# Recalls in four parts, upper weight halves on GpSimd and a new order for the opening of a hybrid decoder kernel

## The reference, cut to what matters

```
h = rmsnorm(x) * norm_pre
c = h @ w_in                       # 1024 -> 3600 columns, split in groups of 256 and a low rank one of 16
A: gated linear attention, 4 heads, log_a = log_sigmoid(a_lr @ gla_w_a2 + b) / 16
C: the same recurrence with k = sigmoid(-c_f), log_f = log_sigmoid(c_f), q = silu(c_q)
   S_t = diag(exp(log_a_t)) S_{t-1} + k_t v_t^T ;  o_t = S_t^T q_t ; o = head_rmsnorm(o)
B: b_b * conv3(b_c * b_v)          D: (trailing means over 2/4/8/16 - d_v) @ pool_w * pool_scale
mix = concat(A, B, C, D), each times silu of its own gate a_z, b_z, c_z, d_z
x = x + rmsnorm(mix @ w_out) * norm_post
```

## Time and profile before

| what | value |
|---|---|
| time, median of 3 runs | 980.12 us (979.66 to 980.3) |
| the profiled execution, its own time | 980.61 us |
| its span, first to last instruction | 978.8 us |
| busy in the span | PE 951.4, DVE 614.2, ACT 431.0, POOL 357.8 us |
| TensorE enters the loop over tiles 2 to 7 | 176.64 us |

### The profile page before, as it was taken

How to read it: one execution, slowest core, us unless ns; L and a number is a source line. 1 busy time by engine, 2 the same in 40 slices (tenths; PEclk the granted TensorE clock), 3 DMA queues, 4 the chain that set the end, 5 groups by cost and what they waited for, 6 DMA issues and landing times.

```text
span 978.8 us, 23985 instructions
## 1 busy us (share of the span) xinstructions
PE 951.4 (97%) x10276; PEld 712.0 (73%) x10276; DVE 614.2 (63%) x1051; ACT 431.0 (44%) x833; POOL 357.8 (37%) x456
## 2 busy tenths in 40 slices
PE   4999999999999999999999999999999999999997
PEld 3777768856887678856887678856887678856783
DVE  5989887437754576537753576537853577447654
ACT  7966355333643334523543434523543435424323
POOL 1315550168004650177103650077103660067300
PEclk9997799999999999999999999999999999999999
DMA  9910432001220104001220104001220013001101
GB/s 332 338 63 3 155 116 72 1 1 45 66 65 2 44 24 109 1 1 44 67 66 1 44 24 108 2 1 45 62 70 1 26 42 87 1 1 45 66 7 44
DMA packets 41547, 56.06 MB, mean 57 GB/s; under 512 B 27808, under 2 KB 28633, under 8 KB 41433
## 3 DMA queue, kind: packets, MB, share of 16 engines
q1 hardware_dynamic: 41441, 54.53, 17.7%
HBM read 38.46 MB, written 9.86 MB: 49 GB/s over the span
## 4 chain that ended last, share of the span: by engine, by line
PE 70%; DVE 14%; ACT 8%; DMA 3%; issue 3%; POOL 1%; SPq 0%; DVEq 0%; ACTq 0%; POOLq 0%
PE pj L873 35%; PE op L1160 16%; PE pj L892 8%; DVE A L2194 3%; PE sc L963 2%; DMA wo_hi<-in_w_units 2%; DVE xres L2087 2%; ACT xres L1501 1%; ACT w_hi L1472 1%; PE sc L1180 1%; PE op L1180 1%; DMA h<-xres 1%; PE m L1072 1%; DVE xres L2448 1%; DVE X L2419 1%
## 5 line engine op out<-in xcount | busy, mean ns | idle before, releaser
L873 PE MATMUL pj<-h,w_hi 128*128 128x256 f16 (+1 forms) x3456 | 385.4, 265 | 3.5 <-DVE w_lo L2065 3.2
L873 PEld LDWEIGHTS pj<-h,w_hi 128*128 128x128 f16 x3456 | 310.6, 99 | 53.5 <-issue 10.0
L873 PE MATMUL pj<-h,w_lo 128*128 128x256 f16 (+1 forms) x1728 | 209.1, 264 | 0.0
L873 PEld LDWEIGHTS pj<-h,w_lo 128*128 128x128 f16 x1728 | 158.2, 99 | 17.5
L2194 DVE COPY_PREDICATED A<-cu8w,sc 64x384 f32<-64x384 uint8 (+1 forms) x168 | 74.0, 440 | 34.6 <-PE sc L963 31.3
L714 POOL TENSOR_TENSOR G<-B 128x256 f32<-128x256 f32 x17 | 12.8, 756 | 176.7 <-DVE B L2120 165.3
L2184 DVE COPY A<-sc 64x256 f32<-64x256 f32 x28 | 11.8, 421 | 87.1 <-PE sc L963 86.9
L892 PE MATMUL pj<-w_hi,h 128*128 128x512 f16 (+1 forms) x272 | 63.3, 379 | 0.0
L730 POOL TENSOR_TENSOR G<-G,Q 128x256 f32<-128x256 f32 x17 | 13.5, 793 | 113.9 <-ACT K L1452 100.0
L2412 DVE SCALAR_TENSOR_TENSOR X<-X 128x512 f32<-128x512 f32 x32 | 22.2, 692 | 50.0 <-ACT X L1452 46.6
L1160 PE MATMUL op<-wo_hi,m_hi 128*128 128x512 f16 x224 | 53.0, 379 | 0.0
(11 more groups left out here) (355 smaller groups left out, 1655.2 us busy)
## 6 DMA issues: line engine op xcount, KB each, us to landing
xin<-in_x_prompt SPq DMA_DIRECT2D x16, 512.0 KB, 4.1
wo_hi<-in_w_units SPq DMA_DIRECT2D x16, 512.0 KB, 7.6
xres<-in_x_prompt SPq DMA_DIRECT2D x15, 512.0 KB, 3.5
out_y_prompt<-xres SPq DMA_DIRECT2D x14, 512.0 KB, 2.6
wo_lo<-in_w_units SPq DMA_DIRECT2D x12, 512.0 KB, 6.6
xres<-in_w_out SPq DMA_DIRECT2D x8, 256.0 KB, 3.1
gpost<-in_w_out SPq DMA_DIRECT2D x8, 256.0 KB, 2.9
m_hi<-in_x_prompt SPq DMA_DIRECT2D x1, 512.0 KB, 5.5
```

Source lines behind the costliest of these rows:

```text
L873: m = pe.matmul(b[:, j * T:(j + 1) * T], w[:, k, col + 128 * j:col + 128 * j + 128], h[:, k, :], start=(n == 0 and k == 0), stop=(n == 2 a ...
```

## The change

Three things. `recall` takes a list of parts, and for tile 0 each of four parts does a quarter of the matmuls, with other work between them. The upper halves of six pieces of w_in (6, 9, 12, 15, 18, 21) are made by GpSimd with a `tensor_scalar` of its own (`upper_helped`), counted by a semaphore of its own; TensorE and SyncE now wait for the lower halves alone, which come after the upper ones. And the lists of all engines for the opening, up to the loop over tiles 2 to 7, are in a new order. The loop and what follows are untouched. The diff, cut where the lists go on in the same manner:

```diff
@@ -69,10 +69,10 @@
 
 def fill_order():
     fills = [
-        (0, "lr"), (0, "la"), (0, "a_k"), (0, "a_q"), (1, "lr"), (1, "la"), (1, "a_q"), (1, "a_k"),
-        (0, "c_f"), (0, "tin"), (0, "vi0"), (0, "c_q"), (1, "c_f"), (1, "c_q"), (0, "d_v"), (1, "vi0"),
-        (0, "d_z"), (1, "vi1"), (0, "po"), (0, "a_z"), (0, "c_z"), (0, "b_c"), (0, "b_v"), (0, "b_z"),
-        (0, "tails"), (0, "b_b"), (1, "d_v"), (1, "d_z"), (1, "po"), (1, "a_z"), (1, "b_c"), (1, "b_v"),
+        (0, "lr"), (0, "la"), (0, "a_k"), (0, "a_q"), (1, "lr"), (1, "la"), (1, "a_q"), (0, "c_f"),
+        (1, "a_k"), (0, "c_q"), (0, "tin"), (1, "c_f"), (0, "vi0"), (0, "d_v"), (1, "vi0"), (1, "c_q"),
+        (0, "d_z"), (0, "po"), (0, "a_z"), (0, "c_z"), (1, "vi1"), (0, "b_c"), (0, "b_v"), (0, "b_z"),
+        (0, "tails"), (0, "b_b"), (1, "d_v"), (1, "d_z"), (1, "po"), (1, "b_c"), (1, "a_z"), (1, "b_v"),
         (1, "b_b"), (1, "b_z"), (2, "lr"), (2, "la"), (1, "c_z"),
...
@@ -140,9 +140,22 @@
     return (0 if name in OWN0 else FIRST.get(name, SIGNALS[name])) + (i - 1) * SIGNALS[name] + k
 
 
+HELPED = (6, 9, 12, 15, 18, 21)
+
+
 def converted(u):
 
     return 2 * u + 2 if u < 4 else u + 5
+
+
+def uppers(u):
+
+    return converted(u) - sum(1 for h in HELPED if h <= u)
+
+
+def helped(u):
+
+    return HELPED.index(u) + 1
 
 
 def needed(col):
...
             def unit(u):
 
                 if u >= NSTAGE:
-                    sp.wait_ge(once["whi"], converted(u - NSTAGE))
                     sp.wait_ge(once["wlo"], converted(u - NSTAGE))
                 sp.dma_start(stage[u % NSTAGE], a["w_units"][u].rearrange("p (k n) -> p k n", k=2)
                              ).then_inc(once["wld%d" % (u % NSTAGE)], 16)
@@ -763,6 +775,14 @@
             k = k_of(i, br)[:, :, 0:T]
             pool.tensor_tensor(k, k, ke_of(i, br)[:, :, 0:T], ALU.mult).then_inc(*give(pool, "kh", i, br + 1))
 
+        def upper_helped(u):
+            k, col = quad(u)
+            pool.wait_ge(*own(pool))
+            pool.wait_ge(once["gs"], 1)
+            pool.wait_ge(once["wld%d" % (u % NSTAGE)], 16 * (u // NSTAGE + 1))
+            pool.tensor_scalar(w_hi[:, k, col:col + 4 * GW], stage[u % NSTAGE].rearrange("p k n -> p (k n)"),
+                               gs[:, k:k + 1], None, ALU.mult).then_inc(*give1(pool, "whp"))
+
         @block.gpsimd
         def _(_pool):
             for hh in range(2):
@@ -770,37 +790,43 @@
             pool.memset(spare[0:T0, 0:192], 0.0).then_inc(*give1(pool, "zero"))
             pool.wait_ge(*own(pool))
             pool.memset(lrb[LRP:LRP + 1, :], 1.0).then_inc(*give1(pool, "zero"))
+            upper_helped(6)
+            upper_helped(9)
+            key_exponents(0, 0)
             exponents(0, 0, LAST)
-            key_exponents(0, 0)
+            upper_helped(12)
             factors(0, 0, LAST)
+            exponents(1, 0, 0)
+            upper_helped(15)
+            upper_helped(18)
+            exponents(1, 0, 1)
+            upper_helped(21)
             key_exponents(0, 1)
-            key_exponents(1, 0)
             exponents(0, 1, LAST)
+            exponents(1, 0, 2)
             key_product(0, 0)
-            exponents(1, 0, 0)
             factors(0, 1, LAST)
-            exponents(1, 0, 1)
+            factors(1, 0, 0)
             key_product(0, 1)
-            factors(1, 0, 0)
             factors(1, 0, 1)
-            exponents(1, 0, 2)
             exponents(1, 0, 3)
             factors(1, 0, 2)
             factors(1, 0, 3)
...
             if i <= 1 and 0 in js:
                 pe.wait_ge(*at("hhi", i, 2 * NC))
                 pe.wait_ge(*at("hlo", i, 2 * NC))
-                pe.wait_ge(once["whi"], needed(col))
                 pe.wait_ge(once["wlo"], needed(col))
             for j in js:
                 for n, (w, h) in enumerate(((w_hi, hi), (w_hi, lo), (w_lo, hi))):
...
                                       a_of(i, hh)[0:C, 2 * c + j, 0:C], start=(c == 0 and j == 0), stop=False, skip_group_check=True)
             m.then_inc(sem("va", i), 1)
 
-        def recall(i, br):
-
-            T, NC, C = dims(i)
-            pe.wait_ge(*at("qt", i, br + 1))
+        def recall(i, br, parts=(0, 1, 2, 3)):
+
+            T, NC, C = dims(i)
+            if 0 in parts:
+                pe.wait_ge(*at("qt", i, br + 1))
             if i == 0:
-                pe.wait_ge(*at("va", i, br + 1))
-                pe.wait_ge(once["smp"], 16 * 2)
-                for j in range(2):
-                    for b in range(DB):
+                if 0 in parts:
...
@@ -1231,94 +1259,100 @@
             transpose_x(1, 0)
             low_rank(0)
             log_alpha(0)
+            transpose_x(1, 1)
             proj(0, "a_k")
-            transpose_x(1, 1)
             proj(0, "a_q")
             low_rank(1)
             log_alpha(1)
             proj(1, "a_q", (0,))
             proj(1, "a_q", (1,))
             proj(1, "a_k", (0,))
+            proj(0, "c_f")
             proj(1, "a_k", (1,))
-            proj(0, "c_f")
+            proj(0, "c_q")
             scores(0, 0, LAST)
+            proj(1, "c_f", (0,))
             tails_in()
+            proj(1, "c_f", (1,))
             values_proj(0, 0)
-            proj(0, "c_q")
-            proj(1, "c_f", (0,))
-            proj(1, "c_f", (1,))
+            proj(0, "d_v")
             transpose_keys(0, 0)
+            values_proj(1, 0, (0,))
+            attend(0, 0)
+            recall(0, 0, (0,))
+            updates(0, 0)
+            values_proj(1, 0, (1,))
+            recall(0, 0, (1,))
+            recall(0, 0, (2,))
+            recall(0, 0, (3,))
+            sample_updates(0)
             proj(1, "c_q", (0,))
             proj(1, "c_q", (1,))
-            attend(0, 0)
-            updates(0, 0)
-            proj(0, "d_v")
-            values_proj(1, 0, (0,))
-            values_proj(1, 0, (1,))
+            scores(0, 1, LAST)
+            head_sums(0, 0)
             proj(0, "d_z")
+            transpose_keys(0, 1)
+            pool_product(0)
+            proj(0, "a_z")
+            attend(0, 1)
+            sample_updates(1)
+            scores(1, 0, 0)
+            proj(0, "c_z")
             values_proj(1, 1, (0,))
-            recall(0, 0)
-            scores(0, 1, LAST)
+            recall(0, 1, (0,))
             values_proj(1, 1, (1,))
-            scores(1, 0, 0)
-            pool_product(0)
-            head_sums(0, 0)
-            proj(0, "a_z")
-            sample_updates(0)
-            transpose_keys(0, 1)
-            proj(0, "c_z")
-            attend(0, 1)
-            recall(0, 1)
+            sample_updates(2)
+            recall(0, 1, (1,))
+            scores(1, 0, 1)
+            recall(0, 1, (2,))
             updates(0, 1)
-            scores(1, 0, 1)
+            recall(0, 1, (3,))
             proj(0, "b_c")
-            sample_updates(1)
+            scores(1, 0, 2)
             head_sums(0, 1)
-            scores(1, 0, 2)
             proj(0, "b_v")
+            scores(1, 0, 3)
             proj(0, "b_z")
-            sample_updates(2)
...
@@ -1795,148 +1829,142 @@
             upper(0)
             upper(1)
             x_hi(1, 0)
-            low_rank_out(0)
             upper(2)
             upper(3)
             x_norm(1, 1)
+            low_rank_out(0)
             upper(4)
             alpha_log(0)
             x_hi(1, 1)
+            upper(5)
             a_key(0)
+            upper(7)
             a_query(0)
-            upper(5)
             low_rank_out(1)
-            upper(6)
-            upper(7)
-            alpha_log(1)
-            level_exp(0, 0, LAST)
             upper(8)
-            upper(9)
             upper(10)
             upper(11)
-            upper(12)
+            alpha_log(1)
+            upper(13)
+            level_exp(0, 0, LAST)
             a_query(1)
-            upper(13)
+            upper(14)
+            forget_log(0)
             key_decays(0, 0)
-            upper(14)
-            a_key(1)
-            upper(15)
-            forget_log(0)
-            tails_copy()
+            decays(0, 0)
             upper(16)
             upper(17)
-            upper(18)
             upper(19)
-            values_out(0, 0)
+            a_key(1)
             upper(20)
-            upper(21)
-            decays(0, 0)
+            tails_copy()
             query_log(0)
-            forget_key(0)
-            key_decays(0, 1)
             upper(22)
             upper(23)
+            query_sigmoid(0)
             upper(24)
-            forget_log(1)
-            query_sigmoid(0)
+            values_out(0, 0)
             upper(25)
             keys_out(0, 0)
-            key_decays(1, 0)
+            forget_key(0)
+            pooling_values(0)
+            forget_log(1)
             upper(26)
-            pooling_values(0)
+            sample_values(0)
+            upper(27)
             values_out(1, 0)
+            square(0, 0)
...
@@ -2496,134 +2527,134 @@
             lower(2)
             lower(3)
```

(55 more changed lines are left out.)

162 lines of the change are left out of this document (84 added, 78 removed).

## The result

The changed kernel takes 986.07 us (median of 4 runs, 985.51 to 988.29) against 980.21 us for the kernel before on the same chip (979.66 to 981.18): ratio 1.0059 with a 95% interval of 1.0047 to 1.0072. It is 5.9 us slower where 2.2 us faster was forecast, and 986.07 lies above the whole range. All three things named as proof of an error happened: VectorE's unbusy time did not shrink, a helped unit takes over 2 us, and the clock falls before 80 us.

A forecast was written before the change was run, and what follows sets the result against it. The opening before the tile loop was taken as bound by TensorE and VectorE together. Terms of +0.2 + 3.5 - 3.7 - 2.3 + 0.1 gave -2.2 us off 980.12: 977.9 us, range 972.5 to 983.

The forecast's parts named there:

- the price of a helped unit: GpSimd's new tensor_scalar of 128x1024: between 0.41 and 3.6 us, taken as 1.3 us each.
- the lock: Rival: each helped unit stops VectorE for its whole length, +7.8 instead of +3.5 us; time 982.2, 985 at 1.8; chance 0.15.
- +3.5 us: Cost on VectorE of helped units 12, 15, 18 and 21 stretching its lower operations, 0.87 us each; ends 0 and 7.8.
- the prediction's sum along VectorE: VectorE's terms, then TensorE from the out product: +0.2 + 3.5 - 3.7 - 2.3 + 0.1 = -2.2 us.
- TensorE's account: Cross-check from TensorE's waits and clock won and waits lost: between -1.6 and -2.6 us, agreeing with the main sum.
- The w_out stage: Reordering pooling(1) and copy_scores around w_out_lower: TensorE's wait at scores(1, 1, 3) mostly covered, +0.1 us.
- worth nothing by itself: Six upper halves leaving ScalarE, 6.4 us: no gain, since ScalarE still waits for VectorE at 62.22 us.
- VectorE's gain of 3.7 us: VectorE's new order to 62 us mostly closes its waits: of 5.7 us not busy, 3.7 won.
- the one of 2.3: From 62 to 105 us, VectorE wins 2.3 of its 5.1 us not busy.
- from 85 to 88 us on: Start of the single expected half-clock stretch, some 12 us instead of 23; clock loss 9.2 us becomes about 5.
- The wait at `sample_updates(0)`: TensorE, there near 60.9 us, waits about 3 us for ScalarE's sample_values(0), ready at 63.8; VectorE loses nothing.
- the clock's early fall: Rival: light matmuls and 3 us idle before proj(1, "c_q") drop the clock near 64 us; +2.8, time 983; chance 0.10.

The follow-up runs named there:

- e11: Changed kernel with each of the six helped units making half its columns (512 of 1024), the other half zeros: 980.61 us, ratio 1.0007.
- e1: Changed kernel with no helped unit, all upper halves back on ScalarE, split recalls and new order kept: 983.03 us, ratio 1.0028.
- e5: e1 with ScalarE's level_exp(1, 1, 0) moved in front of w_out_upper(0): 979.85 us, ratio 0.9996.
- e8: Changed kernel with only units 6 and 9 on GpSimd, 12, 15, 18 and 21 back on ScalarE: 979.87 us, ratio 0.9999.
- e7: Changed kernel, six helped units kept, with forget_sum(0) and query_in(0) ahead of lower(15) on VectorE: 988.66 us, ratio 1.0069.
- e3: Kernel before, with only the recalls of tile 0 split in four parts: 981.76 us, ratio 1.0021.
- e4: Changed kernel with each recall of tile 0 whole again, helped units and order kept: 987.77 us, ratio 1.0079.
- e12: Changed kernel with only the four late units (12, 15, 18, 21) on GpSimd, 6 and 9 back on ScalarE: 984.72 us, ratio 1.0042.
- e10: Kernel before, with only units 6 and 9 made on GpSimd: 980.19 us, ratio 1.0001.
- e2: Kernel before, with only the six upper halves moved to GpSimd, in the old order: 986.94 us, ratio 1.0071.

## Why the prediction was wrong

**The step that failed is the price of a helped unit.** The text took 1.3 us, "near the one-input copy times a little over three", between 0.41 and 3.6. The rows show it at the upper bound: 3.51 to 4.02 us while VectorE works, 2.84 while VectorE stands. The row that it is nearest to was the two-input 1.81 us for half the width (twice that is 3.6), not the small copy; and four times the copy of 128x256, which the width asks for, is already 1.64, not 1.3. And the range did not hold this bound: "the lock" was priced only up to 1.8 us and 985. Six units at 1.3 are 7.8 us of GpSimd, six at 3.6 are 21.7. The first fits into the 33.3 us that GpSimd had free in the earlier trace rows; the second does too by sum, but not by time: unit 15 is wanted at 39.6 us and is made at 43.0. e11 is the test: with units of 2.1 to 2.5 us the loss is down to 0.4 us.

**The price is not all of it.** e1 has no helped unit at all. With the +3.5 us taken out, the prediction's sum along VectorE gives 980.12 - 5.7 = 974.4 us for it, and TensorE's account, which has no such term, some 978; e1 took 983.03. Two more steps failed there. The w_out stage was put at +0.1, and it holds e1's longest wait, 3.0 us before the factors of level 0, branch 1, with half clock behind it; e5's move of one step there gives 3.2 us back. And taking upper halves off ScalarE was called "worth nothing by itself": in the new order the first two are worth 3.2 us (e1 less e8), and VectorE's gain of 3.7 us to 62 us hangs on them. VectorE is not busy there for 5.7 us before, 4.7 in e1 and 1.9 in e8.

**The kind of cost was wrong too.** The prediction put +3.5 us on VectorE as stretched `lower`s. The groups of these lines over the first 200 us, after and then before:

```profile
L2090 DVE SCALAR_TENSOR_TENSOR w_lo<-wo_hi,cf,w_hi 128x1024 f16<-128x1024 f32 x12 | 16.5, 1418 | 1.1 <-ACT w_hi L1506 1.1
L2090 DVE SCALAR_TENSOR_TENSOR w_lo<-wo_lo,cf,w_hi 128x1024 f16<-128x1024 f32 x12 | 16.4, 1401 | 4.5 <-POOL w_hi L783 4.1 <-ACT w_hi L1506 0.4
```

```profile
L2059 DVE SCALAR_TENSOR_TENSOR w_lo<-wo_hi,cf,w_hi 128x1024 f16<-128x1024 f32 x12 | 16.8, 1430 | 0.0
L2059 DVE SCALAR_TENSOR_TENSOR w_lo<-wo_lo,cf,w_hi 128x1024 f16<-128x1024 f32 x12 | 15.0, 1278 | 0.3 <-ACT w_hi L1472 0.2
```

The stretching is 32.9 - 31.8 = 1.1 us against before, whose `lower`s lie beside GpSimd's operations too; against e1, which has the order of after (30.7), it is 2.2. What is new is the 4.1 us in which VectorE waits for GpSimd's product. The prediction counted what a slow neighbour does to VectorE and not that VectorE, in a fixed order, stands for it. The Trainium skill, page "SBUF — State Buffer", section "SBUF: two separate sides", says that the loser of the port pair fully blocks for the whole instruction; by that six units would lay up to 6 x 3.6 = 21.7 us on VectorE (an estimate), and the measured 1.1 or 2.2 us do not bear it out for these forms. That the one that begins second is the longer one does agree (last section).

**A wait was missed in the walk.** Tile 1's `c_f` needs the bank that `query_in(0)` reads, and `query_in(0)` stands behind `lower(15)`. The prediction asked only when `lower(19)` was due. In the kernel after this is TensorE's 5.3 us, and the stretch at half clock behind it. e7 shows that finding this wait alone would not have saved the forecast: others stand next in GpSimd's queue.

**VectorE's gain of 3.7 us came nearly whole with shorter units, the one of 2.3 did not.** In the kernel after, VectorE is not busy for 5.1 us from 18.24 to 62.05 (5.7 before), and most of it is the wait for GpSimd; from 62.05 to 104.79 it is not busy for 6.9 (5.1 before). The same two stretches of e11:

```profile
18.24:62.05 43.81, 40.85 (x516) 31.86 (x516) 41.37 (x50) 30.93 (x61) 31.34 (x25) 1.00 0.75 279
62.05:104.79 42.74, 40.45 (x825) 31.54 (x824) 37.23 (x99) 23.86 (x76) 21.50 (x28) 0.92 0.12 40
```

Not busy are 2.4 and 5.5 us: 3.3 won of the forecast 3.7, and nothing of the 2.3. Its out product starts at 134.56 us, 1.85 before that of the earlier trace rows, where 2.2 was forecast.

**A term was missing: 0.9 us.** The text carried the out product's start to the loop with before's 40.23 us. The new list puts `scores(1, 1, 4)` (the 32 matmuls at 145.36 us above, 0.6 us), which stood ahead of the out product before, behind its first groups, so this distance is 181.20 - 140.07 = 41.13 us, in e11 too. What e11 won by its out product's start is 1.85, 0.6 of it by this move, and 0.95 reaches the loop. By its medians even that is not to be seen: 980.61 against 980.25.

**The clock.** It fell for a shorter time in all, as forecast, but not "from 85 to 88 us on": at 43.9, 101.9 and 119.0. e3 shows that the split does not take the old falls away, and e4 that in the new order whole recalls bring falls near 70 and 94 us that after does not have; "splitting recalls" was neither without effect nor the remedy. The Trainium skill, page "TensorE: Matmul & The Clock Gate", section "What's actually happening", has the clock go down after idle; the fall at 43.9, inside a wait of 5.3 us, agrees, and so may those at 101.9 and 119.0, each behind a wait of 2.0 us; the ones in e3 at 81.0, with TensorE 96% busy ahead of it, and in e4 at 69.8 and 93.7, with TensorE busy throughout, do not. What decides those stays open.

**The wait at `sample_updates(0)`** (3 us forecast, and the clock's early fall as a rival) did not come: its matmuls start at 69.56 us, with no wait in front that the list of waits names. TensorE comes there 8.7 us later than the walk's 60.9, and ScalarE's `sample_values(0)`, begun at 64.7 us, is done by then.

The rival that came nearest, "slower by the lock", had the sign and the operation right and the mechanism wrong; what was not among the rivals is a unit at its upper bound with all that is queued behind it.

What the account of the 5.9 us is, then (medians): helped units 3.0 (after less e1), order with split recalls 2.8 to 3.2 (e1 less before), of which e5 gives 3.2 back by one step. These are parts taken in one sequence; e12 and e8 show that they depend on each other. The four late units are the shown cause: without them (e8), or with units cut to half width (e11), the loss is gone to within 0.4 us.

## What to carry to other kernels

When an operation moves to an engine that is nearly free, its price there is the question, and not the engine's free time: if the trace doesn't show it, run the forecast at both bounds through the whole queue, and let the range reach to what the upper one gives. Cost it as lateness of everything behind it in that engine's order, and of what other engines have queued behind their wait for it, before any contention. Ask also what the relieved engine gives. And offload from the front: in the new order the two units that GpSimd made while it had nothing else were a gain of 3.2 us (none in the old order, e10), and the four among its own steps then cost 6.2 us.

## What the runs showed of the hardware

- GpSimd's `tensor_scalar` with a column of scales, fp32 to fp16, takes 2.84 to 4.63 us for 128x1024, and its length goes with what VectorE runs as it starts. In the 34 instances of the eight traces that have it, the 22 that start well inside a `lower` take 3.51 to 4.63 us; the 12 others, which start with no `lower` under way or in the last 0.2 us of one, take 2.84 to 2.90, one of them 3.32. Two of e2's are below. The first began 0.12 us ahead of four `lower`s, which take 5.75 us where four take 4.85 in the earlier trace rows; the second began inside one:

```profile
23.05 2.85 POOL L783 TENSOR_SCALAR w_hi<-wo_hi,cf 128x1024 f16<-128x1024 f32 x1 [0.97 <-DMA wo_hi<-in_w_units]
...
41.91 4.10 POOL L783 TENSOR_SCALAR w_hi<-wo_hi,cf 128x1024 f16<-128x1024 f32 x1 [1.45 <-DMA wo_hi<-in_w_units]
```

- For 128x512 it takes 2.1 to 2.5 us in e11. Half the width is not half the time: twice the mean of the half, 2.3, less the mean of the whole, 3.6, puts some 1 us on an instruction beside its columns, an estimate from these rows.
- The same operation takes ScalarE 1.06 us, so each of the six cost 2.7 to 3.8 times as much on GpSimd in the kernel after.
- Side by side, VectorE and GpSimd stretch each other by part of an instruction: in the kernel after single `lower`s go from 1.28 to at most 2.14 us, helped units from 2.84 to between 3.51 and 4.02.
- Runs of one kernel differ by up to 9 us (981.19 to 990.01 in e7), where those of the kernel before beside them lie within 3.1 (978.75 to 981.86).
